# A macaron decoder step on one core: the rest of the hidden activations is subtracted on GpSimd and no longer on VectorE

## The reference

```python
def swiglu(h, w_gate, w_up, w_down):
    return (jax.nn.silu(h @ w_gate) * (h @ w_up)) @ w_down

def half_ffn(x, i, k):
    h = rms_norm(x, norm_g[i, 2 * k])
    return x + 0.5 * swiglu(h, ffn_w_gate[i, k], ffn_w_up[i, k], ffn_w_down[i, k])
```

## Time and profile before

| | |
|---|---|
| time, median of 3 runs | 2180.42 us (2180.3 to 2180.65) |
| the profiled execution's own time | 2180.65 us |
| its span, first to last instruction | 2178.9 us |
| PE busy | 2118.2 us, 97% |
| DVE busy | 1526.7 us, 70% |
| ScalarE busy | 994.8 us, 46% |
| POOL busy | 207.7 us, 10% |
| mean granted clock of PE | 0.991 |
| chain of work that ended last | PE 85%, DVE 8%, ACT 3%, POOL 1% |

### The profile page before, as it was taken

One profiled execution on the slowest core, in us unless ns is written; L12 is line 12 of the kernel. 1 busy time (PEld: TensorE's weight loads), 2 busy tenths in 40 slices (PEclk: granted clock), 3 DMA queues, 4 the chain that ended last, 5 costly groups with the idle time before them and its releaser, 6 DMA issues.

```text
span 2178.9 us, 42803 instructions
## 1 busy us (share of the span) xinstructions
PE 2118.2 (97%) x17012; PEld 2042.3 (94%) x17012; DVE 1526.7 (70%) x2222; ACT 994.8 (46%) x1549; POOL 207.7 (10%) x199
## 2 busy tenths in 40 slices
PE   8999999999998999999799999999999998999999
PEld 8999999999998999999799999987668788999999
DVE  7787685335358878597878769577665469787683
ACT  6445363433235535254444536344554445454352
POOL 0100001124031000000000000123121120000000
PEclk9999999999999999999899999999999999999999
DMA  6233233232221323232132322341221112323232
GB/s 182 78 97 116 78 98 114 80 95 74 83 79 59 102 92 116 82 112 97 59 111 92 126 78 96 116 116 36 82 88 59 59 40 78 105 89 122 74 116 76
DMA packets 203635, 198.85 MB, mean 91 GB/s; under 512 B 12071, under 2 KB 200788, under 8 KB 203252
## 3 DMA queue, kind: packets, MB, share of 16 engines
q1 hardware_dynamic: 202938, 196.67, 28.3%
q10 hardware_dynamic: 314, 0.37, 0.1%
q0 software_dynamic: 256, 0.07, 0.0%
HBM read 194.42 MB, written 2.66 MB: 90 GB/s over the span
## 4 chain that ended last, share of the span: by engine, by line
PE 85%; DVE 8%; ACT 3%; issue 2%; POOL 1%; DMA 0%; SPq 0%; DVEq 0%; ACTq 0%; POOLq 0%
PE main L676 35%; PE side L725 21%; PE main L725 16%; PE side L1221 2%; PE main L993 1%; DVE blocks L1859 1%; PE side L1188 1%; DVE w_lo L1710 1%; PE main L1151 1%; PE side L1024 1%; ACT w_hi L1251 1%; DVE w_lo L1737 1%; PE side L1077 1%; PE main L1056 1%; PE side L912 1%
## 5 line engine op out<-in xcount | busy, mean ns | idle before, releaser
L725 PE MATMUL side<-xw_hi,w_hi 128*128 128x260 f32 x1344 | 383.9, 286 | 25.3 <-ACT main L1281 18.0
L676 PE MATMUL main<-h_hi,w_hi 128*128 128x260 f32 x1920 | 387.5, 283 | 4.0 <-DVE x L1877 2.3
L676 PE MATMUL main<-h_hi,w_lo 128*128 128x260 f32 x1920 | 387.1, 283 | 0.0
L676 PE MATMUL main<-h_lo,w_hi 128*128 128x260 f32 x1920 | 386.4, 283 | 0.0
L725 PE MATMUL side<-xw_hi,w_lo 128*128 128x260 f32 x1344 | 381.6, 284 | 0.0
L725 PE MATMUL side<-xw_lo,w_hi 128*128 128x260 f32 x1344 | 380.2, 283 | 0.0
L676 PEld LDWEIGHTS main<-h_hi,w_hi 128*128 128x128 f32 x1920 | 296.3, 189 | 4.9 <-issue 2.7
L676 PEld LDWEIGHTS main<-h_hi,w_lo 128*128 128x128 f32 x1920 | 296.4, 189 | 0.0
L676 PEld LDWEIGHTS main<-h_lo,w_hi 128*128 128x128 f32 x1920 | 295.6, 189 | 0.0
L725 PE MATMUL main<-xw_hi,w_hi 128*128 128x260 f32 x1008 | 288.9, 287 | 2.3 <-DVE tmp_mul L1942 2.3
L725 PE MATMUL main<-xw_lo,w_hi 128*128 128x260 f32 x1008 | 288.4, 286 | 0.0
(11 more groups left out here) (385 smaller groups left out, 3645.0 us busy)
## 6 DMA issues: line engine op xcount, KB each, us to landing
raw<-in_ffn_w_up SPq DMA_DIRECT2D x44, 1024.0 KB, 5.1
raw<-in_ffn_w_gate SPq DMA_DIRECT2D x43, 1024.0 KB, 5.1
raw<-in_ffn_w_down SPq DMA_DIRECT2D x32, 1024.0 KB, 5.2
raw<-in_gmlp_w_in SPq DMA_DIRECT2D x16, 1024.0 KB, 5.4
raw<-in_ffn_w_down SPq DMA_DIRECT2D x16, 768.0 KB, 4.4
raw<-in_gmlp_w_out SPq DMA_DIRECT2D x8, 1024.0 KB, 5.2
raw<-in_mla_w_o SPq DMA_DIRECT2D x8, 1024.0 KB, 5.5
over<-in_cache_mla SPq DMA_DIRECT2D x64, 104.0 KB, 1.9
```

The costliest lines, as they stand in the source:

```text
L676: mm = nc.tensor.matmul(into[:, half, 0:HALF], w[:, k, m * P:(m + 1) * P], moving[:, k, half * HALF:(half + 1) * HALF], start=(k == 0 and ...
L725: mm = nc.tensor.matmul(into[j], w_tiles(w, j)[:, k, :], moving[:, k, j, :], start=(j in (0, 1) and k == 0 and i == 0), stop=(k == 3 and i ...
```

## The change

DVE's `h_rest` is gone, and with it all of its calls: one instruction between two pairs, and two behind a group's last pair. POOL's `h_rest` now does all tiles of all four FFNs, one instruction of 520 elements for each tile; for the pairs that are made in a loop the tile's number is a register, and there the helper also waits for `ws_masked`, which an earlier instruction of POOL sets once. POOL's `ffn` walks the groups and pairs. The semaphores that PE and DVE wait for are counted as before.

```diff
--- before.py
+++ after.py
@@ -1829,13 +1829,6 @@
                 if after == "fast":
                     rest_sums(4, 0, l + 9)
 
-            def h_rest(f, m, n, h):
-
-                dve.wait_ge(h_hi_done, h)
-                at = slice(f, f + n) if isinstance(f, int) else bass.ds(f, n)
-                nc.vector.tensor_tensor(h_lo[:, at, :], tmp_h[:, m:m + n, :], h_hi[:, at, :].bitcast(F32),
-                                        ALU.subtract).then_inc(h_lo_done, n)
-
             def fast_norm(norm, i, part, b, hi, blocks=blocks):
 
                 gains = [gain[:, norm, 2 * i + m:2 * i + m + 1] for m in range(2)]
@@ -1917,12 +1910,7 @@
                         fast_chunk(1, 16 * (n // 2 + i + 2), t + 14 * i + 7, e + 8 * i + 4, l + 10 * i + 5, w + 6 * i + 3,
                                    sn + 6 * i + 3, tmp_h, tmp_act[:, :, :],
                                    "plain" if last else "fast", ready=lambda: dve.wait_ge(act_done, a + 2 * i + 2))
-                        if last:
-                            for m in range(2):
-                                h_rest(2 * i + m + h0, m, 1, h + 2 * i + m + 1)
-                        else:
-                            h_rest(2 * i + h0, 0, 2, h + 2 * i + 2)
-                    h0, rest = 0, pairs
+                    rest = pairs
                     if g == 0 and at.chunk == 0:
                         dve.wait_ge(rms_mm, 1)
                         nc.vector.tensor_copy(halves(rstd_all[:, :]), side[:, 2:4, 0:HALF]).then_inc(rstd_done, 1)
@@ -1956,7 +1944,7 @@
                         for m in range(2):
                             plain_up(1, m, tmp_mul)
                         rest_sums(4, 0, l + 4 + 4)
-                        n, t, e, l, rest, h, a, h0 = n + 4, t + 8, e + 8, l + 4, pairs - 2, h + 4, a + 4, 4
+                        n, t, e, l, rest, h, a = n + 4, t + 8, e + 8, l + 4, pairs - 2, h + 4, a + 4
                         gate_up(0, last=True, n=n, t=t, e=e, l=l, h=h, a=a)
                     else:
                         rest_sums(4, 0, l + 4)
@@ -2405,14 +2393,23 @@
             def h_rest(m, f, h, src=tmp_h):
 
                 pool.wait_ge(h_hi_done, h)
-                nc.gpsimd.tensor_tensor(h_lo[:, f:f + 1, :], src[:, m:m + 1, :], h_hi[:, f:f + 1, :].bitcast(F32),
-                                        ALU.subtract).then_inc(h_lo_done, 1)
+                if not isinstance(h, int):
+                    pool.wait_ge(ws_masked, 1)
+                nc.gpsimd.tensor_tensor(h_lo[:, bass.ds(f, 1), :], src[:, m:m + 1, :],
+                                        h_hi[:, bass.ds(f, 1), :].bitcast(F32), ALU.subtract).then_inc(h_lo_done, 1)
 
             def ffn(at, after, final=False):
-                if at.chunk == 0:
-                    for i in range(2):
+                h = at.h
+                for g, pairs in enumerate(FF_GROUPS):
+                    plain = 2 if g == 0 and at.chunk == 0 else 0
+                    for i in range(plain):
                         for m in range(2):
-                            h_rest(m, 2 * i + m, at.h + 2 * i + m + 1, (tmp_h, tmp_mul)[i])
+                            h_rest(m, 2 * i + m, h + 2 * i + m + 1, (tmp_h, tmp_mul)[i])
+                    with pool.Fori(0, pairs - plain) as i0:
+                        i = i0 + plain
+                        for m in range(2):
+                            h_rest(m, 2 * i + m, h + 2 * i + m + 1)
+                    h += 2 * pairs
                 if not final:
                     for k in range(KD):
                         add_squares(k % 2, after.sums - KD + k, k == 0)
```

## The result

The changed kernel takes 2215.07 us (median of 4 runs, 2213.74 to 2217.39) against 2180.36 for the kernel before beside it (4 runs, 2177.79 to 2180.65). The ratio is 1.0163, 95% interval 1.0145 to 1.018: slower by 35 us. The forecast was 2206.4, with a range of 2190 to 2220.

What follows compares the result with a forecast made beforehand. PE was taken as the bound, with DVE's L1811 close behind. 24.0 us between pairs plus 2.0 at group ends made 26.0 on the profiled 2180.65: 2206.65, as a median 2206.4; range 2190 to 2220.

Steps and rivals of the forecast that it cites:

- the slack of 0.25 us at position 6: First chunk of a pair: L1811 can end 0.25 us later before PE must wait for it at position 6.
- 54 instructions less on DVE are worth nothing by themselves: DVE's removed subtractions: 30 between pairs, 1.16 us each, only offset POOL's cost; 24 at group ends gain nothing.
- Two POOL instructions take 2 x 1.08 from DVE, less 1.16: Between two pairs: POOL's SBUF reads hold DVE up, making L1811 1.05 us late after the 1.16 saved.
- the credit: Between two pairs: the 1.16 us DVE saves by the removed subtraction, forecast as eaten by POOL's first instruction.
- The term, 30 x 0.80 = 24.0: At 30 boundaries between pairs PE waits 0.80 us at position 6, 24.0 us in all; bounds 22.5 to 34.5.
- 0.5 at the ends of the 3-pair groups: At the end of one group per FFN, PE waits 0.5 us for POOL's h_lo, 4 times: 2.0 us.
- Everything after PE is shifted with it; PE's own instructions are the same.: After each PE stall: later work moves by the same time, no later wait takes it back, nothing is added.
- The estimate by the page's ratio, about 27 us: Between pairs: with GpSimd at 1.96 times VectorE, a subtraction holds the port 1.37 us, the term about 27 us.
- Rival (a): Between pairs: POOL gets in only where DVE uses PSUM or pauses; stall 0.5, term 15, 2197.4 us; chance 0.12.
- Rival (b): Between pairs: L1811 shifts by less than 0.25 us, only the group ends cost, 2182.4 us; chance 0.12.
- Rival (c): At the 30 boundaries: each stall drops PE's clock, 30 x 2.4 + 2 = 74 us, 2254 us; chance 0.05.

Runs made afterwards that it cites:

- e6_early: The changed kernel, but in a pair's first chunk DVE does L1811 ahead of the rest of 1024 elements that stood before it; 2188.14 us (ratio 1.004).
- e3_memset: The changed kernel, but between pairs POOL writes zeros to h_lo instead of subtracting; group ends still subtracted on POOL; 2188.79 us (ratio 1.0043).
- e1_ends: Against the kernel before: POOL takes over only the subtractions behind each group's last pair, DVE keeps those between pairs; 2189.71 us (ratio 1.0042).
- e2_between: Against the kernel before: POOL takes over only the 60 subtractions between pairs, DVE keeps those at group ends; 2208.36 us (ratio 1.0135).

## Why the prediction was right, step by step

- **What bounds it, and the slack of 0.25 us at position 6.** Right. PE waits for L1811 at position 6 of the first chunk, 30 times more, and nowhere else in the pair. L1811 is 1.09 late and the pair 0.84 longer; the difference is the slack. e6_early takes this wait away and leaves the rest alone.
- **54 instructions less on DVE are worth nothing by themselves.** Right: e3_memset has them off DVE as well (30 of them with no contention in their place), its DVE is busy for 0.93 us less in the pair than before (17.69 against 18.62), and its pair still takes 20.20.
- **Two POOL instructions take 2 x 1.08 from DVE, less 1.16.** Right in size: +1.00 and +1.12 less 1.04. I had the first one eat the credit before L1747 starts and the second strike the rest. In the trace the first strikes L1747 itself (it is sent at 277.70, while POOL's first runs to 278.83). That is the same time booked to another row. The rows beforehand gave 1.05 late, 1.09 was measured. The term, 30 x 0.80 = 24.0, came out as 24.8.
- **0.5 at the ends of the 3-pair groups.** 0.57 to 0.70, 2.7 for 2.0. At the first of them POOL's second subtraction ends 93.51 + 1.30 = 94.81; ScalarE is 1.62 later there than before (its two h_hi start at 91.53 for 89.91), so on the old scale that is 93.19, for a forecast of 93.2. The wait on a counter in a register with its loop arithmetic, put at 0 to 0.4 us for want of a row, comes out at 0.12: the ends of the three FFNs where a loop does these subtractions cost 0.69 or 0.70 in the changed kernel, and 0.58 in e1_ends, where no loop does.
- **"Everything after PE is shifted with it; PE's own instructions are the same."** This is the step that failed in size. The same instructions took about 8 us more (8.1 on the mean; 8.5 in the one trace, of which 7.0 are clock), for which the sum had no term; it put the clock at full and unchanged. Without it the forecast is 26.0 for 25.9 (time at full clock) or 27.5 (one trace). The measured 2215.07 lies 8.7 above the forecast of 2206.4. The range holds it because its upper end allowed for a dearer contention, which didn't come; that this room was as large as the loss of clock is luck.
- **The estimate by the page's ratio, about 27 us.** It is summed wrongly: a subtraction longer by 0.09 comes twice at a boundary, so it would give 30 x 0.98 = 29.4. The measured 24.8 goes with the duration from the trace (1.28), not with the ratio.
- **Rival (a), POOL not let in between two DVE instructions:** wrong; the rest of 512 elements is hit at 279.84, at once behind L1747, and L1737 after L1806 has its 1.21.
- **Rival (b), not slower:** wrong; DVE lost 2.1 a boundary, and 1.41 was the point from which it decides.
- **Rival (c), each stall drops the clock:** wrong as put. The granted clock is 1.00 over the pair with its stall, and e2_between with 24 us of stalls loses no more clock than kernels without. I had looked for the clock only where the change puts its stalls, and the loss turned up in other stretches, of the gMLP, the MLA and the starts of FFNs.

## What to carry to other kernels

Before moving elementwise work from VectorE to an idle GpSimd, count SBUF inputs: where both engines read two tensors from SBUF, each GpSimd instruction (here 1.28 us) makes VectorE stand still for about 1.1 us and takes only 0.6 us of work off it. Both prices are those of this subtraction and these shapes. Then look not at busy shares but at the next instruction on which the bounding engine waits: 0.25 us of slack there turned 1.09 us into 0.84 a time, and one instruction placed earlier turned it into nothing. And keep a few microseconds in the range for the granted clock in stretches that the edit doesn't touch.

## What was not expected of the hardware

- GpSimd and VectorE take turns, instruction by instruction, when both have work ready: the first subtraction held L1747, the second waited for it (278.83 to 281.08, for work of 1.28) and held the next rest, though VectorE had work ready throughout. Each is lengthened, VectorE by 1.00 to 1.12 us and GpSimd by 0.66 and 0.97 (276.89 to 278.83 and to 281.08, for 1.28 each).
- A GpSimd memset of the same tile took 0.53 us and cost VectorE nothing.
- A kernel with one VectorE instruction moved, and the same mean span at full clock (2160.5 us), ran 6 us longer, by its granted clock (0.9882 for 0.9912, 6 and 17 runs). The cause wasn't found. Against effects of this size, the time at full clock was the number in which the experiments could be compared.
